# Mask, log-count and bias: added by TensorE before the row maximum, or by VectorE in it

## The reference, cut to what matters

```python
# attn0: 16 instances (selected and window branch of 8 heads) with a causal mask,
#        8 heads with a 128 wide causal window and a sink logit
s = jnp.where(mask, s, -jnp.inf); m = max(s); p = exp(s - m); den = sum(p) (+ exp(sink - m))
# attn1: 16 heads, three dilated patterns merged by their denominators. At 256 tokens this
#        is one softmax with log(count) added, count = how many patterns see the key
# attn2: 8 heads of 2-D neighbourhood attention: s = s + rpb[...]  (window and bias)
#        8 heads of plain attention, nothing added
# attn3: 8 differential and 8 latent-attention heads, nothing added
o = (p / den) @ v
```

## Time and profile before

| | us |
|---|---|
| median of 3 runs (1077.7 to 1082.21) | 1079.36 |
| profiled execution, its own time | 1080.68 |
| its span, first to last instruction | 1078.8 |
| PE busy / DVE busy / ACT busy / POOL busy | 969.0 / 662.0 / 483.2 / 179.9 |
| mean granted TensorE clock | 0.938 of full |
| attn0, first score to last weighted matmul | 102.9 to 170.6 |
| attn1 | 463.5 to 512.1 |
| attn2 | 823.2 to 875.8 |

### The profile page before, as it was taken

One profiled execution on the slowest core, in us unless ns is written; L12 is line 12 of the kernel. 1 busy time (PEld: TensorE's weight loads), 2 busy tenths in 40 slices (PEclk: granted clock), 3 DMA queues, 4 the chain that ended last, 5 costly groups with the idle time before them and its releaser, 6 DMA issues. The chain is left out here.

```text
span 1078.8 us, 15064 instructions
## 1 busy us (share of the span) xinstructions
PE 969.0 (90%) x5804; PEld 818.0 (76%) x5804; DVE 662.0 (61%) x1097; ACT 483.2 (45%) x891; POOL 179.9 (17%) x129
## 2 busy tenths in 40 slices
PE   5995878899999999988899999998998789886778
PEld 4794546799998888855699999886886468676556
DVE  5697783555556468646455565546871857867672
ACT  5362552455455345345344455434542635343550
POOL 2003020000000000131000000003654300407540
PEclk9996888899999999988989999998998999898899
DMA  8481002365566656510536656656852025443001
GB/s 317 131 257 75 1 1 79 115 198 176 177 211 199 189 167 210 176 59 1 156 118 194 196 158 204 214 168 158 256 173 78 1 64 176 147 140 134 1 1 39
DMA packets 96791, 148.71 MB, mean 138 GB/s; under 512 B 6272, under 2 KB 59680, under 8 KB 96592
## 3 DMA queue, kind: packets, MB, share of 16 engines
q1 hardware_dynamic: 94512, 140.50, 41.0%
q10 hardware_dynamic: 1296, 4.83, 1.3%
q0 software_dynamic: 912, 2.41, 1.0%
HBM read 146.67 MB, written 1.05 MB: 137 GB/s over the span
## 5 line engine op out<-in xcount | busy, mean ns | idle before, releaser
L889 DVE TENSOR_TENSOR w_lo<-w_raw,w_hi 128x1024 fp32r<-128x1024 f32 (+2 forms) x230 | 272.8, 1210 | 152.4 <-ACT w_hi L600 148.7
L600 ACT ACTIVATE w_hi<-w_raw 128x1024 fp32r<-128x1024 f32 (+2 forms) x269 | 273.5, 1042 | 169.6 <-DMA w_raw<-in_w_gate_up 74.7
L1466 PE MATMUL ps<-hT_hi,w_lo 128*128 128x256 f32 x832 | 240.1, 289 | 8.1 <-POOL w_lo L492 4.6
L1467 PE MATMUL ps<-hT_hi,w_hi 128*128 128x256 f32 x832 | 239.4, 288 | 0.0
L1468 PE MATMUL ps<-hT_lo,w_hi 128*128 128x256 f32 x832 | 239.2, 287 | 0.0
L1466 PE MATMUL ps<-w_hi,hT_lo 128*128 128x512 f32 (+3 forms) x448 | 173.7, 388 | 8.1 <-DVE w_lo L889 4.4
L1466 PEld LDWEIGHTS ps<-hT_hi,w_lo 128*128 128x128 f32 x832 | 163.9, 197 | 9.4 <-issue 6.5
L1468 PE MATMUL ps<-w_lo,hT_hi 128*128 128x512 f32 (+3 forms) x448 | 170.7, 381 | 0.0
L1467 PE MATMUL ps<-w_hi,hT_hi 128*128 128x512 f32 (+3 forms) x448 | 170.5, 381 | 0.0
L1467 PEld LDWEIGHTS ps<-hT_hi,w_hi 128*128 128x128 f32 x832 | 163.9, 197 | 0.0
L1468 PEld LDWEIGHTS ps<-hT_lo,w_hi 128*128 128x128 f32 x832 | 163.9, 197 | 0.0
(11 more groups left out here) (213 smaller groups left out, 1192.8 us busy)
## 6 DMA issues: line engine op xcount, KB each, us to landing
w_raw<-in_w_gate_up SPq DMA_DIRECT2D x176, 256.0 KB, 4.4
w_raw<-in_w_down SPq DMA_DIRECT2D x44, 512.0 KB, 4.4
w_raw<-in_w_in_e SPq DMA_DIRECT2D x38, 512.0 KB, 5.1
w_raw<-in_w_qkv_o SPq DMA_DIRECT2D x24, 512.0 KB, 3.8
w_raw<-in_w_in_o SPq DMA_DIRECT2D x20, 512.0 KB, 3.6
w_raw<-in_w_out_e SPq DMA_DIRECT2D x16, 512.0 KB, 4.6
w_raw<-in_w_out_o SPq DMA_DIRECT2D x16, 512.0 KB, 3.5
w_raw<-in_w_in_e SPq DMA_DIRECT2D x8, 268.0 KB, 2.7
```

What stands on the lines that cost most here:

```text
L600: n.activation(w_hi[:, u % RING, 0:size], w_raw[:, u % RING, 0:size], ACT.Copy).then_inc(hi_ready, 1)
L889: v.tensor_tensor(w_lo[:, u % RING, 0:size], w_raw[:, u % RING, 0:size], w_hi[:, u % RING, 0:size].bitcast(F32), ALU.subtract).then_inc(lo ...
L1466: m.matmul(o, lhs[1], rhs[0], start=start, stop=False)
L1467: m.matmul(o, lhs[0], rhs[0], start=False, stop=False)
```

## The change

VectorE's row maximum and the addition become one instruction, `tensor_tensor_reduce`, which reads the scores from PSUM and the addend from SBUF, writes minus the sum to `prob`, and the minimum of that (the negated maximum) to `negm`. The matmuls with the identity go. The exponential reads `prob` in place, with scale -1, in place of PSUM. So the wait for the transposes of s-3 moves from ACT to DVE for these instances (and so does attn2's wait for the bias rows, from TensorE), and TensorE may overwrite a bank once its maximum is there, not its exponentials. The early copies and their tiles go. The semaphores of the six layer norms are folded into four with running counts; each wait has the same meaning as before. Core of the diff:

```diff
-    mask_b = place("mask_b", [P, 2, 384], BF16)
-    ident_b = place("ident_b", [P, P], BF16)
-    ident_r = place("ident_r", [P, P], F32R)
-    logc = place("logc", [P, 2, 384], F32R)
...
+    def mask_rows(m):
+        return lambda t: masks[:, m, P * t:P * t + P * (t + 1)]
+
+    def bias_rows(h):
         def f(t):
             row = bias_na[:, h, 2 - 2 * t, 63:64]
-            return [(ident, bass.AP(row.tensor, row.offset, [row.ap[0], [64, 4], [-1, 64]]))]
+            return bass.AP(row.tensor, row.offset, [row.ap[0], [64, 4], [-1, 64]])
         return f
...  ACT, attention
                     act.wait_ge(max_ready, i + 1)
-                    if s >= 3:
+                    if s >= 3 and it["bias"] is None:
                         act.wait_ge(t_filled, f0 + s - 2)
                     w = P if it["causal"] else T
-                    n.activation(prob[:, i % 3, 0:w], ps[:, i % 3, 0:w], ACT.Exp, bias=negm[:, i, 0:1],
-                                 accum_out=den[:, i, 0:1])
+                    src, sign = (ps, 1.0) if it["bias"] is None else (prob, -1.0)
+                    n.activation(prob[:, i % 3, 0:w], src[:, i % 3, 0:w], ACT.Exp, bias=negm[:, i, 0:1],
+                                 scale=sign, accum_out=den[:, i, 0:1])
...  ACT, early
-        n.activation(ident_b[:, :], ident, ACT.Copy)
-        n.activation(ident_r[:, :], ident, ACT.Copy)
-        n.activation(mask_b[:, :, :], masks[:, 0:2, :], ACT.Copy)
-        n.activation(logc[:, 0, :], masks[:, 2, :], ACT.Copy).then_inc(sem("narrow"), 1)
...  DVE, attention
-                    if it["causal"]:
-                        v.tensor_reduce(out=negm[:, i, 0:1], in_=logits[:, 0, 0:P], axis=AX.X, op=ALU.max, negate=True)
-                        ins = v.tensor_reduce(out=negm[:, i, 1:2], in_=logits[:, 1, :], axis=AX.X, op=ALU.max,
-                                              negate=True)
+                    if it["bias"] is not None:
+                        if s >= 3:
+                            dve.wait_ge(t_filled, f0 + s - 2)
+                        if stage == "attn2":
+                            dve.wait_ge(sem("bias_ready"), s + 1)
+                        for t in range(NT):
+                            w = P * (t + 1) if it["causal"] else T
+                            out_, in_, row = (prob[:, i % 3, 256 * t:256 * t + w], logits[:, t, 0:w], it["bias"](t))
+                            if not it["causal"]:
+                                out_, in_ = (b.rearrange("p (u c) -> p u c", u=4) for b in (out_, in_))
+                            ins = v.tensor_tensor_reduce(out=out_, in0=in_, in1=row, scale=-1.0, scalar=-4.0 * NEG,
+                                                         op0=ALU.add, op1=ALU.min, accum_out=negm[:, i, t:t + 1])
...  DVE, early
-        link(v.tensor_tensor(logc[:, 1, :], masks[:, 2, :], logc[:, 0, :].bitcast(F32), ALU.subtract))
...  TensorE, scores
             for e in two:
-                if e >= 3:
+                if e >= 3 and inst[e - 3]["bias"] is None:
                     pe.wait_ge(exp_ready, i0 + e - 2)
-                if stage == "attn2" and e < 8:
-                    pe.wait_ge(sem("bias_ready"), e + 1)
+                elif e >= 3:
+                    pe.wait_ge(max_ready, i0 + e - 2)
...
-                    for n_, (idm, b) in enumerate(it["bias"](t) if it["bias"] is not None else []):
-                        m.matmul(o, idm, b, start=n_ == 0, stop=False)
...
-                    ins = m.matmul(o, it["q"][:, t * P:(t + 1) * P], it["k"][:, 0:w], start=it["bias"] is None,
-                                   stop=True)
+                    ins = m.matmul(o, it["q"][:, t * P:(t + 1) * P], it["k"][:, 0:w], start=True, stop=True)
```

More of the change, by code:

```diff
@@ L256, in net, with norm_sem, norm_at @@
     H1, HT, KC, VC, CS = 2, 1, 6, 7, 2
+    NORM_ORDER = {0: 0, 1: 1, 2: 2, 3: 3, 5: 4, 6: 5}
+    NORM_EVENTS = {"ss": 4, "ms": 2, "rstd": 2, "h": 4}
+    def norm_sem(what, k):
+        return sem(f"norm4_{what}" if k == 4 else f"norm_{what}")
+    def norm_at(what, k):
+        return 0 if k == 4 else NORM_ORDER[k] * NORM_EVENTS[what]
     slot_full = [sem(f"slot_full_{s}") for s in range(RING)]
@@ L354, in instances @@
                     out.append(dict(q=pair_row("prep0", "qr", h), k=dup_row("prep0", kk, h // 4, h),
-                                    bias=mask_passes(0), v=(z0, vlo + HD * (h // 4), HD), causal=True, half=h % 2,
+                                    bias=mask_rows(0), v=(z0, vlo + HD * (h // 4), HD), causal=True, half=h % 2,
                                     pair=h // 2, first=False, last=br == 1, gate=(h, br + 1)))
@@ L358, in instances @@
                 out.append(dict(q=pair_row("prep0", "bq", h), k=dup_row("prep0", "bk", h // 4, h),
-                                bias=mask_passes(1), v=(z0, 1944 + HD * (h // 4), HD), causal=True, half=h % 2,
+                                bias=mask_rows(1), v=(z0, 1944 + HD * (h // 4), HD), causal=True, half=h % 2,
                                 pair=4 + h // 2, first=True, last=True, sink=h))
@@ L362, in instances @@
             for h in range(16):
-                out.append(dict(q=pair_row("prep1", "q", h), k=pair_row("prep1", "k", h), bias=count_passes,
+                out.append(dict(q=pair_row("prep1", "q", h), k=pair_row("prep1", "k", h), bias=mask_rows(2),
                                 v=(z1, 2048 + HD * h, HD), causal=True, half=h % 2, pair=h // 2, first=True,
@@ L367, in instances @@
             for h in range(8):
-                out.append(dict(q=pair_row("prep2", "qa", h), k=pair_row("prep2", "ka", h), bias=bias_passes(h),
+                out.append(dict(q=pair_row("prep2", "qa", h), k=pair_row("prep2", "ka", h), bias=bias_rows(h),
                                 v=(z2, 1024 + HD * h, HD), causal=False, half=h % 2, pair=h // 2, first=True,
@@ L606, in load_gain @@
             if wait is not None:
-                act.wait_ge(sem(f"norm{wait}_h"), 4)
+                act.wait_ge(norm_sem("h", wait), norm_at("h", wait) + 4)
             act.dma_start(gb[:, :] if dst is None else dst, src.partition_broadcast(P))\
@@ L695, in attention @@
                     act.wait_ge(max_ready, i + 1)
[L696 removed]
+                    if s >= 3 and it["bias"] is None:
                         act.wait_ge(t_filled, f0 + s - 2)
                     w = P if it["causal"] else T
[L699 to L702 removed]
+                    src, sign = (ps, 1.0) if it["bias"] is None else (prob, -1.0)
+                    n.activation(prob[:, i % 3, 0:w], src[:, i % 3, 0:w], ACT.Exp, bias=negm[:, i, 0:1],
+                                 scale=sign, accum_out=den[:, i, 0:1])
+                    n.activation(prob[:, i % 3, 256:512], src[:, i % 3, 256:512], ACT.Exp, bias=negm[:, i, 1:2],
+                                 scale=sign, accum_out=den[:, i, 1:2]).then_inc(exp_ready, 1)
                     if "sink" in it:
@@ L1606, in scores @@
                     o = ps[:, i % 3, 256 * t:256 * t + w]
-                    for n_, (idm, b) in enumerate(it["bias"](t) if it["bias"] is not None else []):
-                        m.matmul(o, idm, b, start=n_ == 0, stop=False)
-                for e in two:
-                    it, i = inst[e], i0 + e
-                    w = P * (t + 1) if it["causal"] else T
-                    o = ps[:, i % 3, 256 * t:256 * t + w]
-                    ins = m.matmul(o, it["q"][:, t * P:(t + 1) * P], it["k"][:, 0:w], start=it["bias"] is None,
-                                   stop=True)
+                    ins = m.matmul(o, it["q"][:, t * P:(t + 1) * P], it["k"][:, 0:w], start=True, stop=True)
                     if t == NT - 1:
```

34 lines of the change are left out of this document (13 added, 21 removed).

## The result

| | before | after |
|---|---|---|
| median, same chip, 4 runs each (us) | 1078.63 | 1051.22 (1047.26 to 1055.33) |
| ratio, 95% interval | 1 | 0.974 (0.9695 to 0.9785) |
| profiled execution, its time (us) | 1080.68 | 1052.18 |
| PE / DVE / ACT busy (us) | 969.0 / 662.0 / 483.2 | 934.8 / 664.3 / 484.5 |
| granted TensorE clock | 0.938 | 0.946 |

The forecast was 1063 with a range of 1055 to 1075. TensorE lost its 34 us of busy time, and VectorE, which does the additions now, is no busier than before (664.3 us against 662.0).

What follows compares the result with a forecast made beforehand. No one engine bounds throughout: TensorE and VectorE tie in attn0, VectorE has room in attn1 and attn2. Terms -7.5 (attn1), -7.5 (attn2), -1.0 (attn0) sum to -16.0: 1064.7 from the profiled 1080.7, 1063 us against the median; range 1055 to 1075.

Steps and rivals of the forecast that it cites:

- the price of the accumulator read: VectorE, after each new maximum: 0.1 us a read (bounds 0 to 0.2), four a pair, 0.4 us per pair.
- rival 3: VectorE's new instruction is slow, taking twice its reduction and bounding the kernel everywhere: 1088 us; chance 0.07.
- Rival 2: The accumulator read on VectorE is free: 6.5 us more gained, 1056 us; chance 0.10.
- what GpSimd's units cost in attn2: attn2, first maximum to fifth pair: two units hold VectorE at 1.8 us each, 3.6 of 20.35 us.
- The pace itself: attn2's three later pair intervals: 4.65 us each, from attn1's 3.8 plus 0.9 for wider tiles.
- the least certain term: attn0, 12 pairs: earlier pairs gain, pairs where VectorE is full lose; -1.0 us in sum.
- rival 4: Gain hidden by GpSimd collisions and the clock, or new instruction also waits for GpSimd: 1076 to 1082 us; chance 0.05.
- 1, the clock falls: TensorE, with less work, is granted half clock in the attention stages: 9 us back, 1072 us; chance 0.14.
- One sign of being wrong: TensorE at L1659 waiting longer for scaled probabilities than the 1.44 us it did once would show the forecast wrong.
- the early copies: Between 28 and 40 us, where TensorE is always busy: removing them counted at nothing, at most 0.56 us.

Runs made afterwards that it cites:

- linked_dose: Changed kernel plus one 12-column VectorE write ahead of each of 48 instances' fused instructions, which wait for it by a semaphore: 1061.20 us, ratio 0.9816.
- after_again: The changed kernel itself run and profiled once more, unedited, to show how far one profile's stages repeat: 1051.76 us, ratio 0.9729.
- small_ahead: Changed kernel plus a small VectorE memset of 128x12 ahead of each of the 96 new instructions, without a semaphore: 1051.91 us, ratio 0.9724.

## Why the prediction was wrong

**The step that failed first: the price of the accumulator read.** The prediction says "No row shows tensor_tensor_reduce" and, of the accumulator read, "no VectorE row here shows it", and it took 0.1 us a read from ACT's 196 ns. Both sentences are false. The trace of before has the instruction, by another name, later in the program, where lines 1323 and 1329 are tensor_tensor_reduce calls (DVE timeline of the kernel before):

```profile
910.94 0.42 DVE L1323 CUSTOM_DVE_ANT_0 tmp<-z 128x256 f32<-128x256 f32 x1
911.29 0.08 DVE L1323 DVE_READ_ACCUMULATOR2_ANT small<- 128x1 f32 x1
911.40 0.29 DVE L1323 CUSTOM_DVE_ANT_0 tmp<-z 128x128 f32<-128x128 f32 x1
911.62 0.08 DVE L1323 DVE_READ_ACCUMULATOR2_ANT small<- 128x1 f32 x1
...
912.75 0.22 DVE L1329 CUSTOM_DVE_ANT_0 tmp<-gains 128x64 f32<-128x64 f32 x1
912.90 0.08 DVE L1329 DVE_READ_ACCUMULATOR2_ANT small<- 128x1 f32 x1
```

The numbers were there: 0.42 and 0.29 us for 256 and 128 columns, and a read of 0.08 that starts 0.35 and 0.22 after its instruction, about where the next one of a free run would start. By the prediction's own rule, that an instruction starts 0.08 us before the end of the one ahead, a read of 0.08 costs nothing. (These calls are linked by semaphores, so only the trace of after shows the next instruction start beside the read.) That takes rival 3 off the list before anything is run. It also bears on the rule that the prediction quoted from the Trainium skill ("Vector Engine (DVE) Microarchitecture Reference", "Points that are easy to get wrong"), half throughput with two SBUF sources that are not bf16: L1323 has two f32 sources in SBUF (the same rows of z twice) and an accumulator, and takes the 0.42 us of the form with one source in PSUM; L1329 has two different ones, and its 0.22 us for 64 columns lie on the same line. Whether these calls are of the shape that the page names, no row shows. The cost of the error, in the prediction's own terms: 0.4 us in each of seven pairs of attn0's sum (3 at full clock, 4 where DVE is full), 2.8; 0.4 in each of attn1's seven intervals and 0.2 at its end, 3.0; 0.4 in each of attn2's four intervals, 1.6. That is 7.4 us, measured at 0, and linked_dose shows that time which VectorE is really charged does come out in the total. Without it the forecast is about 1056. Rival 2 ("the read is free") had the mechanism and 1056.

**The second: what GpSimd's units cost in attn2.** The prediction put 4.65 us on each of three pairs, and 1.8 us on each of two collisions with GpSimd: 20.35 us from the first maximum to the fifth pair. It took 15.82. The four intervals are 2.67, 3.43, 5.01 and 4.71 us, where 2.8 and then 4.65 three times were forecast, plus the collisions. The two GpSimd units of this stretch, and a third right behind it, with the VectorE scaling that each of them met (after):

```profile
813.49 2.36 POOL L492 TENSOR_TENSOR w_lo<-w_raw,w_hi 128x1024 fp32r<-128x1024 f32 x1 [9.47 <-ACT w_hi L600]
815.25 0.75 DVE L1065 TENSOR_SCALAR prob<-prob,fac 128x256 f32<-128x256 f32 x1
...
817.77 2.45 POOL L492 TENSOR_TENSOR w_lo<-w_raw,w_hi 128x1024 fp32r<-128x1024 f32 x1 [1.93 <-ACT w_hi L600]
819.57 0.80 DVE L1065 TENSOR_SCALAR prob<-prob,fac 128x256 f32<-128x256 f32 x1
...
822.09 2.48 POOL L492 TENSOR_TENSOR w_lo<-w_raw,w_hi 128x1024 fp32r<-128x1024 f32 x1 [1.87 <-ACT w_hi L600]
822.27 2.44 DVE L1066 TENSOR_SCALAR prob<-prob,fac 128x256 f32<-128x256 f32 x1
```

A scaling alone takes 0.35. So the first two units cost 0.85 us together and not 3.6: most of their time passed beside maxima and copies with an operand in PSUM, which they don't hold, and beside idle time. The third met a scaling at its start and cost 2.1 by itself. The price of such a unit is not a constant; it is what is left of it when VectorE reaches its next operation from SBUF to SBUF. Of the 4.5 us that the forecast of this stretch was off, these are 2.75 and the reads 1.6. The pace itself, 4.65 less 0.4 of reads, was about right. The last three intervals less their collisions are 3.43, 4.6 and 4.3 us, 4.1 in the mean. The first is short because no output is complete yet; the second has 0.77 us of idle time ahead of a copy.

**attn0, "the least certain term".** It was -1.0, and the reads inside it are 2.8 us (the 4.8 that the prediction names are all 48 of attn0, more than it let into its sum). Without them it is -3.8. Measured: -5.7, and -3.8 in the repeat, whose clock was 0.72 in attn0 against 0.78. The three pairs at full clock took 3.40 us each where 3.8 had been forecast and 3.63 was the pace before: that is the reads. The second to fourth pairs opened 1.3, 1.0 and 0.3 us sooner after the one ahead, where 1.2, 0.9 and 0.3 were forecast. The 2 us by which the first profile lies below -3.8 are the last stretch shown above, where the clock was 1.00 in place of 0.73. The forecast has no term for that, and no run shows whether it belongs to the change. So it is partly luck that the repeat comes out at -3.8 to the tenth: its last stretch gave back 0.9 us as well, and its fourth pair opened 0.45 us later than before.

**attn1.** The first maximum came earlier as forecast. The pace was (486.98 - 457.41) / 7 = 4.22 us, 4.8 forecast; less the reads' 0.4 the forecast is 4.4. The collisions were there as it said: four units, 5.9 us above their own length (forecast 7.2), and those 1.3 us over seven intervals bring 4.4 down to the 4.2 measured. One of them, in after_again:

```profile
466.96 2.47 POOL L492 TENSOR_TENSOR w_lo<-w_raw,w_hi 128x1024 fp32r<-128x1024 f32 x1 [8.36 <-ACT w_hi L600]
467.13 0.28 DVE L1017 CUSTOM_DVE_ANT_0 prob<-ps,table 128x128 f32<-128x128 f32 x1
...
467.33 0.42 DVE L1017 CUSTOM_DVE_ANT_0 prob<-ps,table 128x256 f32<-128x256 f32 x1
...
467.99 1.52 DVE L1065 TENSOR_SCALAR prob<-prob,fac 128x128 f32<-128x128 f32 x1
...
469.83 0.55 PE L1654 MATMUL ps<-table,prob 128*128 128x128 f32 x3 [1.16 <-DVE prob L1066]
```

GpSimd starts; the new instruction, with one operand in PSUM, keeps its length; the scaling from SBUF to SBUF ends within 0.1 us of GpSimd, and TensorE's transposes have stood idle for 1.16 us when they start. Of 96 new instructions none exceeds 0.425 us, so the part of rival 4 that let it wait for GpSimd is out. In this the engines do not meet at semaphores alone: no semaphore stands between L492 and L1065.

**The rivals.** 1, the clock falls: it did not in attn1 (0.79 before, 0.82 and 0.90 after), and in attn0 it is what sets one profile apart from the next (0.78 before, 0.78 and 0.72 after). 3, slow instruction: out. 4, hidden: out. 2 was right in its mechanism and had 0.10; its 1056 is still 5 us above what was measured. One sign of being wrong did show: TensorE waited up to 1.9 us at L1654 for scaled probabilities in attn1, above the 1.44. But the kernel before has one wait of 1.9 at that place too, so the sign could not tell the two apart.

**What held.** One pass at 290 and 415 ns; L1608 gone from TensorE; the first maximum of attn2 3.9 us earlier (forecast 4.0); the early copies worth nothing, within the 1 to 2 us that the parts between scatter; DVE's idle time behind the scores down from 16.2 to 3.5 us in attn1; the wait for the exponentials small. Of the 12 us missed the reads are about 7, and the collisions, cheaper than priced, about 4 (2.75 in attn2, 1.3 in attn1). The rest is within the scatter of the stages.

## What to carry to other kernels

Before an operation is called unseen, look for its call in the whole source and read the rows of those lines: the profile names a fused reduction CUSTOM_DVE, and a search by operation misses it. Before a collision is priced, look at what the held engine will have queued while the other runs: the same GpSimd unit cost VectorE 0.40 us at one place and 2.1 at another. And an engine that is idle a third of a stage can still be on its path: in the kernel before, taking 2 us collisions away from VectorE gained more than the engine's share let one expect, and in the changed kernel taking work off it (copies to ScalarE, low halves away from GpSimd) was worth 20 us more.

## What the runs showed of the hardware

- The accumulator read of a fused reduction on VectorE, 82 ns long, costs nothing between starts (0.00 us behind 85 of 96 in after; the next one waits for a result behind the others).
- A small VectorE write next to an independent instruction costs 0.02 us between starts: 68 ns long, it starts 0.01 us beside its neighbour (small_ahead). With a semaphore between them it costs 0.14 us (linked_dose).
- GpSimd's 2.35 us subtraction holds VectorE operations from SBUF to SBUF (up to 2.44 us for 0.35), until it ends, and not those with an operand in PSUM (none of 96 above 0.425 us). The Trainium skill, "GPSIMD Engine Reference", "Key points", has VectorE instructions with two SBUF inputs or in a two-port mode contend with GpSimd; the trace agrees, and shows it for a scaling with one SBUF tensor (L1065).
- Doing such a unit on VectorE itself takes 1.22 us, half of GpSimd's 2.35, and less than most collisions with it cost in attn0 and attn1 (1.1 to 2.2 us above the operation's own length).
